# A float32 product with a column of ones, or two products of rounded parts: the gates of a modulated two-layer block

## The reference

```
m   = silu(c) @ ada_w[i] + ada_b[i]          # 6 parts of 1024: shift, scale, gate; shift, scale, gate
h   = rms_norm(x, g0) * (1 + m[1]) + m[0]
x   = x + m[2] * rms_norm(mixer(h), g1)      # part 2 is a gate
h   = rms_norm(x, g2) * (1 + m[4]) + m[3]
x   = x + m[5] * rms_norm(mlp(h), g3)        # part 5 is a gate
```

## Time and profile before

| | |
|---|---|
| median of 3 runs | 1995.83 us |
| the profiled execution | 1995.16 us, span 1993.3 us |
| PE busy | 1954.5 us (98%) |
| DVE, ACT, POOL busy | 1390.3 (70%), 885.7 (44%), 254.6 us (13%) |
| granted TensorE clock | 0.997 of 2.4 GHz |

### The profile page before, as it was taken

One profiled execution on the slowest core, in us unless ns is written; L12 is line 12 of the kernel. 1 busy time (PEld: TensorE's weight loads), 2 busy tenths in 40 slices (PEclk: granted clock), 3 DMA queues, 4 the chain that ended last, 5 costly groups with the idle time before them and its releaser, 6 DMA issues.

```text
span 1993.3 us, 27409 instructions
## 1 busy us (share of the span) xinstructions
PE 1954.5 (98%) x10285; PEld 1619.2 (81%) x10285; DVE 1390.3 (70%) x2220; ACT 885.7 (44%) x1513; POOL 254.6 (13%) x333
## 2 busy tenths in 40 slices
PE   7999999999999999999999999999999999989998
PEld 3877788788888777888889888878888878878887
DVE  5899767788766645488987665766755467566655
ACT  3433354333333453575554224524333353556554
POOL 2101011111111200411101001011110021321000
PEclk9999999999999999999999999999999999999999
DMA  8434225655653540378865432545555245227753
GB/s 307 133 100 134 85 96 180 201 181 178 195 177 96 172 159 22 108 232 282 262 206 161 135 109 74 198 147 171 167 171 157 68 154 180 81 98 232 223 184 110
DMA packets 191859, 315.19 MB, mean 158 GB/s; under 512 B 14653, under 2 KB 114328, under 8 KB 191728
## 3 DMA queue, kind: packets, MB, share of 16 engines
q1 hardware_dynamic: 162512, 210.09, 32.7%
q0 software_dynamic: 29216, 103.36, 17.0%
HBM read 312.35 MB, written 1.05 MB: 157 GB/s over the span
## 4 chain that ended last, share of the span: by engine, by line
PE 90%; DVE 4%; issue 2%; ACT 1%; POOL 1%; DMA 1%; SPq 0%; POOLq 0%; DVEq 0%; ACTq 0%
PE bank L683 26%; PE bank L690 24%; PE bank L689 24%; PE bank L693 9%; PE bank L688 2%; PE bank L686 2%; PE bank L738 1%; PE bank L762 1%; DVE acc L2203 1%; DVE wl L2178 1%; DMA raw<-in_ada_w 1%; PE bank L1068 0%; POOL wl L3111 0%; ACT junk L1579 0%; DVE X L2314 0%
## 5 line engine op out<-in xcount | busy, mean ns | idle before, releaser
L1563 ACT ACTIVATE wh<-raw 128x1024 fp32r<-128x1024 f32 (+4 forms) x390 | 399.4, 1031 | 593.7 <-PE bank L690 556.6
L2178 DVE TENSOR_TENSOR wl<-raw,wh 128x1024 fp32r<-128x1024 f32 (+3 forms) x372 | 440.0, 1189 | 266.5 <-ACT wh L1563 265.1
L683 PE MATMUL bank<-HH,wh 128*128 128x256 f32 (+1 forms) x1552 | 516.5, 333 | 2.9 <-DVE HH L2297 2.0
L690 PE MATMUL bank<-HH,wl 128*128 128x512 f32 (+1 forms) x1232 | 415.1, 337 | 0.0
L689 PE MATMUL bank<-HL,wh 128*128 128x512 f32 (+1 forms) x1232 | 414.9, 337 | 0.0
L2203 DVE SCALAR_TENSOR_TENSOR acc<-ada,sc,acc 128x512 f32<-128x512 f32 x518 | 362.2, 745 | 2.3
L683 PEld LDWEIGHTS bank<-HH,wh 128*128 128x128 f32 x1552 | 294.5, 190 | 32.0 <-issue 6.0
L683 PE MATMUL bank<-wh,UH 128*128 128x512 f32 x768 | 306.5, 399 | 0.0
L689 PE MATMUL bank<-wl,UH 128*128 128x512 f32 x768 | 303.3, 395 | 0.0
L690 PE MATMUL bank<-wh,UL 128*128 128x512 f32 x768 | 303.2, 395 | 0.0
L689 PEld LDWEIGHTS bank<-HL,wh 128*128 128x128 f32 x1232 | 232.5, 189 | 27.7 <-issue 2.2
(11 more groups left out here) (348 smaller groups left out, 2596.4 us busy)
## 6 DMA issues: line engine op xcount, KB each, us to landing
raw<-in_mlp_w SPq DMA_DIRECT2D x256, 512.0 KB, 4.4
ada<-in_mod_w POOLq DMA_DIRECT2D x96, 512.0 KB, 4.7
ada<-in_ada_w POOLq DMA_DIRECT2D x80, 512.0 KB, 4.6
raw<-in_ml_w_qkvo SPq DMA_DIRECT2D x28, 512.0 KB, 3.9
raw<-in_conv_w_in SPq DMA_DIRECT2D x24, 512.0 KB, 4.5
raw<-in_ada_w SPq DMA_DIRECT2D x12, 512.0 KB, 6.2
raw<-in_mla_w_o SPq DMA_DIRECT2D x8, 512.0 KB, 4.0
raw<-in_gla_w_v SPq DMA_DIRECT2D x8, 512.0 KB, 3.9
```

The lines of the kernel that those rows point to most:

```text
L683: pe.matmul(o, sh, mh, start=start, stop=False, skip_group_check=True)
L690: return pe.matmul(o, sl, mh, start=False, stop=stop, skip_group_check=True)
L1563: act.activation(k.wh[n % NSPL][:, 0:m], k.raw[(NDIRECT + n) % NRAW][:, 0:m], ACT.Copy).then_inc(*k.w_hi.up("w hi", n))
L2178: dve.tensor_tensor(k.wl[n % NSPL][:, 0:m], k.raw[(NDIRECT + n) % NRAW][:, 0:m], k.wh[n % NSPL][:, 0:m].bitcast(F32), ALU.subtract).then_i ...
```

## The change

A gate's sum is split as weights are: ACT rounds `acc` to float32r into `Gh`, DVE subtracts it from `acc` in place and leaves the rest in `accl`, and PE adds two rounded products with the ones in one bank. `Gh` lies in the memory of `G`, `accl` in that of `acc`. The three steps stand one, two and four steps behind the half's last piece, where the product stood three behind. The biases of a new layer are turned one piece later. Where a gate is wanted at once before its rest is made, `whole` drops the two first steps and sums it unrounded as before. The constant of ones is float32r now and made by DVE from the identity instead of loaded by POOL.

```diff
@@ ada_units
-                elif part == 0 and ch == 0 and kk == 1:
+                elif part == 0 and ch == 0 and kk == 2:
                     end = ("columns", li)
@@ Walk.step
         elif end is not None:
-            self.closing.append([self.lag, key, end])
+            if end[0] == "finish" and end[2] in (2, 5):
+                self.closing.append([1, key, ("leading",) + end[1:5] + (False,)])
+                self.closing.append([2, key, ("low",) + end[1:5] + (False,)])
+                self.closing.append([4, key, end])
+            else:
+                self.closing.append([self.lag, key, end])
@@ Walk.ensure
                 else:
+                    self.whole()
                     self.flush(9)
+    def whole(self):
+        whole = [end[1:4] for _, _, end in self.closing if end[0] == "low"]
+        closing, self.closing = self.closing, []
+        for n, key, end in closing:
+            if end[1:4] not in whole:
+                self.closing.append([n, key, end])
+            elif end[0] == "finish":
+                self.closing.append([n, key, end + (True,)])
@@ lay_out
+        with ExitStack() as s1:
+            self.G = sb("G", [128, 2, D], F32, s1)
+        self.Gh = sb("Gh", [128, 2, D], F32R)
...
+        self.accl = sb("accl", [128, 2, 2, 512], F32R)
...
+        self.ones = sb("ones", [128, 128], F32R)
@@ pe_program, close
-                    mm(b[:, :], k.ones[:], k.acc[:, n % 2, ty, :]).then_inc(*b.filled())
+                    if len(c) == 7:
+                        mm(b[:, :], k.ones[:].bitcast(F32), k.acc[:, n % 2, ty, :]).then_inc(*b.filled())
+                        ps.give(b)
+                        continue
+                    w.wait_ge(*at("sum hi", n, ty))
+                    mm(b[:, :], k.ones[:], k.Gh[:, ty, ch * 512:ch * 512 + 512], True, False)
+                    w.wait_ge(*at("sum lo", n, ty))
+                    mm(b[:, :], k.ones[:], k.accl[:, n % 2, ty, :], False, True).then_inc(*b.filled())
@@ act_program, close
+        if c[0] == "leading":
+            li, part, ch, types = c[1:5]
+            n = CHUNK[li, part, ch]
+            w.wait_ge(*at("ada sum", n, 3))
+            for ty in types:
+                if (ch, ty) in gate_before:
+                    for t in range(2):
+                        w.wait_ge(*at("gated", *gate_before[ch, ty], ch, ty * 2 + t))
...
+                act.activation(k.Gh[:, ty, ch * 512:ch * 512 + 512], k.acc[:, n % 2, ty, :],
+                               ACT.Copy).then_inc(*k.sum_hi.up("sum hi", n, ty))
@@ dve_program, close
+        if c[0] == "low":
...
+                w.wait_ge(*at("sum hi", n, ty))
+                dve.tensor_tensor(k.accl[:, n % 2, ty, :], o, k.Gh[:, ty, ch * 512:ch * 512 + 512].bitcast(F32),
+                                  ALU.subtract).then_inc(*k.sum_lo.up("sum lo", n, ty))
@@ dve_program, first instruction
+    w.wait_ge(*at("ident"))
+    dve.tensor_scalar(k.ones[:], k.ident[:], 0.0, 1.0, ALU.mult, ALU.add).then_inc(*own.up("ones"))
@@ pool_program, first instruction
-    pool.dma_start(k.ones[:], k.cap("ones")).then_inc(*k.ones_in.up("ones", by=16))
```

More of the change, by code:

```diff
@@ L466, in __init__ @@
         self.blocks = list(weight_stream(A))
-        self.ident_in, self.ones_in, self.c_in = sig("ident_in"), sig("ones_in"), sig("c_in")
+        self.ident_in, self.c_in = sig("ident_in"), sig("c_in")
         self.x_in = [sig(f"x_in{t}") for t in range(4)]
@@ L483, in __init__ @@
         self.ada_sum, self.bias_cols, self.mod_done, self.gate_rows = sig("ada_sum"), sig("bias_cols"), sig("mod_done"), sig("gate_rows")
+        self.sum_hi, self.sum_lo = sig("sum_hi"), sig("sum_lo")
         self.mean_in, self.rstd_in = sig("mean_in"), sig("rstd_in")
@@ L514, in lay_out @@
         self.Y4 = self.Y[:, 0:4096].rearrange("p (t n) -> p t n", t=4)
-        self.G = sb("G", [128, 2, D])
+        with ExitStack() as s1:
+            self.G = sb("G", [128, 2, D], F32, s1)
+        self.Gh = sb("Gh", [128, 2, D], F32R)
         self.raw = [sb(f"raw{i}", [128, 1024]) for i in range(NRAW)]
@@ L519, in lay_out @@
         self.ada = [sb(f"ada{i}", [128, 2, 512]) for i in range(NADA)]
-        self.acc = sb("acc", [128, 2, 2, 512])
+        with ExitStack() as s1:
+            self.acc = sb("acc", [128, 2, 2, 512], F32, s1)
+        self.accl = sb("accl", [128, 2, 2, 512], F32R)
         self.gb = sb("gb", [128, 2, 512])
         self.drow = [[self.G[0:2, ch, part * 512:part * 512 + 512] for part in range(2)] for ch in range(2)]
-        self.ident, self.ones = sb("ident", [128, 128]), sb("ones", [128, 128])
+        self.ident = sb("ident", [128, 128])
+        self.ones = sb("ones", [128, 128], F32R)
         self.ta = Ring([sb(f"ta{i}", [128, 512]) for i in range(2)], at)
@@ L740, in close @@
                     for m in range(4):
-                        p = mm(b[:, i * 4 + m:i * 4 + m + 1], k.acc[:, n % 2, ty, m * 128:m * 128 + 128], k.ones[:, 0:1])
+                        p = mm(b[:, i * 4 + m:i * 4 + m + 1], k.acc[:, n % 2, ty, m * 128:m * 128 + 128], k.ones[:, 0:1].bitcast(F32))
                 p.then_inc(*b.filled())
@@ L1566, in unit @@
         pass
+    gate_before = {}
     def close(c):
-        pass
+        if c[0] == "leading":
[6 more added lines that the diff above has]
+                        w.wait_ge(*at("gated", *gate_before[ch, ty], ch, ty * 2 + t))
+                else:
+                    for half in range(2 if ch == 0 else 1):
+                        w.wait_ge(*ps.of("dcol", ch, half).full())
+                gate_before[ch, ty] = li, part
+                act.activation(k.Gh[:, ty, ch * 512:ch * 512 + 512], k.acc[:, n % 2, ty, :],
+                               ACT.Copy).then_inc(*k.sum_hi.up("sum hi", n, ty))
     walk = Walk(len(k.blocks), split, unit, close)
@@ L1875, in log_gates @@
                 g = k.gx[:, r, t, :]
-                act.activation(g, g, ACT.Ln, bias=k.ones[:, 0:1]).then_inc(*k.log_act.up("log act", r, t))
+                act.activation(g, g, ACT.Ln, bias=k.ones[:, 0:1].bitcast(F32)).then_inc(*k.log_act.up("log act", r, t))
         def q_out(n):
@@ L2018, in gates @@
             w.wait_ge(*at("ones"))
-            act.activation(k.mfa[:], k.mfa[:], ACT.Ln, bias=k.ones[:, 0:1]).then_inc(*own.up("forget log"))
+            act.activation(k.mfa[:], k.mfa[:], ACT.Ln, bias=k.ones[:, 0:1].bitcast(F32)).then_inc(*own.up("forget log"))
         def rows(r):
@@ L2239, in close @@
     def close(c):
-        if c[0] == "columns":
+        if c[0] == "low":
+            n, ch, types = CHUNK[c[1:4]], c[3], c[4]
+            for ty in types:
+                o = k.acc[:, n % 2, ty, :]
+                w.wait_ge(*at("ada sum", n, 3))
+                w.wait_ge(*at("sum hi", n, ty))
+                dve.tensor_tensor(k.accl[:, n % 2, ty, :], o, k.Gh[:, ty, ch * 512:ch * 512 + 512].bitcast(F32),
+                                  ALU.subtract).then_inc(*k.sum_lo.up("sum lo", n, ty))
+        elif c[0] == "columns":
             b = ps.of("cols", c[1])
@@ L2244, in close @@
         elif c[0] == "finish":
-            li, part, ch, types, last = c[1:]
+            li, part, ch, types, last = c[1:6]
             if part in (2, 5):
```

## The result

The changed kernel took 1985.70 us (median of 4 runs, 1984.81 to 1986.74), the kernel before 1996.59 beside it. The ratio of the two is 0.9948, with a 95% interval of 0.9937 to 0.9959: 8.2 to 12.6 us less, 10.4 in the middle. A second set of runs of the unaltered change gave 0.9948 again (0.9936 to 0.9961). The profiled execution took 1986.48 us with a span of 1984.7, so 8.7 us less than that of before; the forecast was 8.5 less, 1987.3 us.

What follows compares the result with a forecast made beforehand. TensorE's own stream was taken to bound the kernel (90% of the chain). Gates -8.9, late tile +0.3 and bias turn +0.1 gave -8.5 us from the median 1995.83, so 1987.3 us; range 1984.8 to 1992.

Steps and rivals of the forecast that it cites:

- The products: On PE, 22 of 24 gates as two rounded products at 0.227 us each instead of 0.857 a gate: 8.9 us less.
- Both bounds of the price: Price of a new gate product on PE: at least a weight load, 0.19 us; at worst a float32 pass, 0.43 us.
- The hidden work: Added roundings, 14.6 us on ACT, and subtractions, 15.2 us on DVE, charged nothing; bounds 0 to 29.8 us.
- My covers: PE's arrival less the subtraction's end: 3 us or more at thirteen of fourteen places, thinnest there at layer 3's first gate.
- Layer 0's second half: Part 2 of layer 0, wanted at once: second low part ready 0.5 us or more before PE asks; no wait.
- rival (c): ACT stands on the addition's end, delaying weight roundings and evictions; 1 us at fifteen places reaches PE: 2002 us, chance 0.06.
- The late tile: Layer 0, second half: gate bias and gain tile loads later, delaying gating 0.6 to 2.3 us; charged 0.3, bounds 0 and 2.3.
- The bias turn of layer 1: Bias rows wait for a later gate, landing at 378.8 against PE at about 379.2; charged 0.1 us, bounds 0 and 2.
- The start: DVE makes the constant from the identity in idle time; taken as zero, between 0.2 us gain and 0.7 loss.

## Why the prediction was right

**The products.** 22 x 0.403 = 8.9 us was forecast. The pair fell from 1.71 to 0.91 us, and undoing the products alone gave 9.0 us of steps. Both bounds of the price were off the mark and the nearest row was it: 0.227 us. The lower one, the time of a weight load, was no bound. Among products of 256 columns in the kernel before, the loads of 0.19 us overlap and start 0.12 us apart, as the products do:

```profile
736.18 0.19 PEld L690 LDWEIGHTS bank<-HH,wl 128*128 128x128 f32 x1
736.30 0.19 PEld L683 LDWEIGHTS bank<-HH,wh 128*128 128x128 f32 x1
```

The rule of the Trainium skill (Perfetto Trace Analysis, Identifying the Most-Contended Engine) that spoke against the gain, the share of weight loads as a measure of TensorE, did not decide here: loads stayed at 1618.9 us (1619.2 before) while the time fell.

**The agreement with one execution.** 8.7 us between the profiles, 8.5 forecast: part of that is luck. I had read the clock as at its upper level throughout, from 40 slices of some 50 us, which do not show drops of a few us. Comparing starts, the gates give 8.75 us and all else nets to nothing, but it is made of drops of the clock at different places, three in each profile beside the one at the end. Before had them at 44 to 52, 1752 to 1760 and 1800 to 1808, after at 44 to 52, 188 to 196 and 860 to 868, (1 - 0.79) x 8 = 1.7 us each, so they cancel between these two profiles; nothing in the forecast made them do so. Two rows of before:

```profile
188.00:196.00 8.00, 7.46 (x27) 5.11 (x28) 7.33 (x23) 2.58 (x8) 0.73 (x1) 1.00 0.37 124
...
1800.00:1808.00 8.00, 6.83 (x43) 6.52 (x42) 6.54 (x11) 5.86 (x11) 0.64 (x1) 0.79 0.91 299
```

**The hidden work.** ACT and DVE were 12.9 and 11.9 us busier, where I had said 14 to 16. The additions themselves were 13.5 and 14.4; other groups got shorter by some, and I did not follow which. PE's busy time fell by 7.6, just under the 8 to 10 I gave. PE waits for no part. My covers were wrong at two places: I said 3 us or more in thirteen. Layer 3's first gate has 2.7 us (3.1 said), and I overlooked layer 1, part 5, second half, where DVE ends at 942.62 and PE asks for the low part at 944.85, 2.2 us. The run with the old place shows that these two, and layer 0's first pair, need the fourth piece.

**Layer 0's second half.** Cover 0.5 us was said, and more in fact; it was 2.2. DVE, ACT and PE there, as in the earlier trace rows:

```profile
250.32 1.29 DVE L2294 TENSOR_TENSOR accl<-acc,Gh 128x512 fp32r<-128x512 f32 x2
254.63 0.69 DVE L2308 TENSOR_TENSOR G<-bank,gb 128x512 f32<-128x512 f32 x1 [3.03 <-DMA gb<-in_norm_g]
```

```profile
246.64 1.16 ACT L1616 ACTIVATE Gh<-acc 128x512 fp32r<-128x512 f32 x2 [4.01 <-DVE acc L2251]
247.92 1.06 ACT L1595 ACTIVATE wh<-raw 128x1024 fp32r<-128x1024 f32 x1
```

```profile
253.78 0.39 PE L718 MATMUL bank<-accl,ones 128*128 128x512 f32 x1
```

The low parts are made by 251.6, and PE takes the second at 253.78. ACT stands 4.0 us on the addition, as rival (c) said, and its next block slips to 247.92, but no wait of PE follows: (c) had the stand right and the price wrong. The late tile came as predicted: DVE waits 3.0 us for it and begins the second half's G at 254.63. That is 0.13 past my 252.5 to 254.5, in an execution that a drop of the clock at 188 had put 1.2 us behind; in the second one, without that drop, it is 251.45, 1.05 ahead of it. But the 0.3 us that I charged for it was nothing: PE's pause ahead of the next hidden tile (`HH`), at 284, is 0.54 us in both kernels.

```profile
283.98 0.36 PE L708 MATMUL bank<-HH,wh 128*128 128x256 f32 x1 [0.54 <-issue]
```

**The bias turn of layer 1.** Charged at 0.1 us, it cost nothing: PE turns the biases at 377.00 without a wait, as in the earlier trace rows, and the rows had landed at 375.6. I had placed PE 1.4 to 2.2 us and the rows 3.2 us too late. The margin, 1.4 us, is thin: the run with the dearer side work used it up.

```profile
377.00 0.26 PE L742 MATMUL bank<-ident,gb 48*128 48x48 f32 x1
```

**The start.** DVE makes the constant at 2.69 in 0.46 us, long before its next instruction at 4.93. Taken as zero, and the run without the parts agrees (0.9996).

**What stays open.** The runs put the change at 10.4 us, with 8.2 to 12.6 inside the interval; the gates explain 8.75 to 9.0. Whether the rest is more than scatter can't be told from these runs. No version tried here that keeps both parts of the sum beats the changed kernel; the one with the leading product alone is faster by what it leaves out.

## What to carry to other kernels

A float32 product against an exact constant can be had in two rounded ones at about half of TensorE's time (0.454 us against 0.857 here), if the roundings fit into idle time of other engines and end before TensorE comes. Count that margin in the planner's own unit: here a piece was from under one block to nearly three. Place the consumer late rather than early, since one wait of 2.15 us, with the drop of the clock behind it, gave back what nearly ten gates saved (3.9 us against 0.40 each). Sum in one go what is wanted at once. And follow what waits for a moved step: the bias rows had a thinner margin (1.4 us) than any part (2.2).

## What the runs showed of the hardware

A wait of TensorE can cost more than itself. With the 2.58 and 1.32 us waits of the dearer side work, the granted clock fell to the 1.2 GHz level (0.50 from 256 to 260), and the products came 3.2 us later than the waits explain; behind the 4.12 us wait for the biases, 1.6 us. In the run with the gates two pieces behind, 13 of the 14 waits, of 2.84 to 8.79 us, came with such a drop, and the profile is 30 us longer than those waits explain. It is not so every time: the 14th wait, 2.91 us, had no drop, nor had the waits of 1.34, 1.35 and 2.58 us in the run with three pieces. In the one profile with TensorE kept at work through the 4 us wait, the clock stood at 1.00 in that stretch. Pauses of 1 to 2 us that the kernel has anyway are followed by such a drop in some executions and not in others; from one profile to the next most of these drops stand elsewhere. Two profiles of this kernel can therefore differ by a few us at places that a change doesn't touch; comparing the starts of the same products, place by place, tells these from the change.
